# Bias products moved to the middle of an expert loop, and two late loads cut in halves

## The reference

```python
logits = (x2d @ w_router) + b_router
top_logits, top_idx = lax.top_k(logits, TOP_K)
gates = jax.nn.softmax(top_logits, axis=-1)
gu = xe @ w_gu[e] + b_gu[e]            # 1024 x 2048 per expert
g = jnp.minimum(gu[:, :D_FF], 7.0)
u = jnp.clip(gu[:, D_FF:], -7.0, 7.0)
h = (u + 1) * (g * jax.nn.sigmoid(1.702 * g))
y = h @ w_down[e] + b_down[e]          # 1024 x 1024 per expert
out = zeros.at[row_token].add(y * gate)
```

## Time and profile before

| | |
|---|---|
| median of three runs | 1069.88 us |
| profiled execution | 1070.29 us |
| its span | 1068.5 us |
| PE busy | 1024.9 us, 96% |
| DVE busy | 331.3 us, 31% |
| ACT busy | 92.6 us, 9% |
| from HBM | 418.29 MB |
| PE waiting for weights of `w_gu` | 32.1 us in 16 waits |

### The profile page before, as it was taken

The page is one execution under the profiler, slowest core; times in us unless marked ns, Lnnn a source line. Parts: engine busy times, 40 slices in busy tenths (PEclk is TensorE's granted clock), DMA queues, the critical chain, the costliest instruction groups (busy, mean ns, idle before and its releaser), DMA issues.

```text
span 1068.5 us, 11798 instructions
## 1 busy us (share of the span) xinstructions
PE 1024.9 (96%) x5098; PEld 490.2 (46%) x5099; DVE 331.3 (31%) x571; ACT 92.6 (9%) x162; POOL 8.3 (1%) x20
## 2 busy tenths in 40 slices
PE   9999999999999999989898989989898989999998
PEld 7767454444444444444343534344343435334333
DVE  3533031243323232323223241323223232413243
ACT  2222030010000000000000010100000000100001
POOL 1100000000000000000000000000000000000000
PEclk9999999999999999999999999999999999999999
DMA  9970969999999999999999999999999999999996
GB/s 351 302 193 3 370 255 401 421 421 411 418 425 429 428 424 429 428 426 430 429 426 429 429 427 429 429 427 429 429 427 429 428 427 429 427 416 420 421 420 240
DMA packets 60499, 420.39 MB, mean 393 GB/s; under 512 B 21396, under 2 KB 21712, under 8 KB 28848
## 3 DMA queue, kind: packets, MB, share of 16 engines
q1 hardware_dynamic: 59872, 419.32, 95.1%
q0 software_dynamic: 352, 0.55, 0.2%
q10 hardware_dynamic: 240, 0.03, 0.0%
HBM read 418.29 MB, written 1.58 MB: 393 GB/s over the span
## 4 chain that ended last, share of the span: by engine, by line
PE 74%; DMA 25%; SPq 0%; issue 0%; DVE 0%; ACT 0%; DVEq 0%
PE ps L911 36%; DMA ring<-in_w_gu_dram 25%; PE ps L927 9%; PE ps L837 8%; PE ps L759 5%; PE ps L953 4%; PE ps L777 3%; PE ps L635 2%; PE ps L938 1%; PE ps L913 1%; PE ps L788 1%; PE ps L957 1%; PE ps L1089 1%; PE ps L661 1%; PE ps L727 0%; PE ps L704 0%
## 5 line engine op out<-in xcount | busy, mean ns | idle before, releaser
L911 PE MATMUL ps<-ring,xT 128*64 128x512 f32 x1008 | 451.9, 602 | 32.1 <-DMA ring<-in_w_gu_dram 31.8
L913 PE MATMUL ps<-ring,xT 128*64 128x512 f32 x1000 | 449.2, 602 | 0.0
L911 PEld LDWEIGHTS ps<-ring,xT 128*64 128x64 f32 x1008 | 134.8, 138 | 303.1 <-issue 298.8
L927 PE MATMUL ps<-ring,he 128*64 128x512 f32 x472 | 210.3, 595 | 3.6 <-DMA ring<-in_w_down_dram 2.8
L929 PE MATMUL ps<-ring,he 128*64 128x512 f32 x472 | 210.8, 596 | 0.0
L1675 DVE TENSOR_TENSOR acc<-ps,acc 128x512 f32<-128x512 f32 (+1 forms) x78 | 50.4, 684 | 276.2 <-PE ps L953 248.5
L913 PEld LDWEIGHTS ps<-ring,xT 128*64 128x64 f32 x1000 | 133.8, 138 | 0.0
L927 PEld LDWEIGHTS ps<-ring,he 128*64 128x64 f32 x472 | 61.9, 137 | 131.4 <-issue 131.2
L837 PEld LDWEIGHTS ps<-oh,x 128*128 128x128 f32 x768 | 95.3, 196 | 10.3 <-issue 7.4
L837 PE MATMUL ps<-oh,x 128*128 128x128 f32 x768 | 97.9, 283 | 0.0
L1318 ACT COPY gu_sb<-ps 128x1024 f32<-128x1024 f32 x16 | 16.2, 1012 | 585.1 <-PE ps L913 585.1
(11 more groups left out here) (236 smaller groups left out, 645.2 us busy)
## 6 DMA issues: line engine op xcount, KB each, us to landing
ring<-in_w_gu_dram SPq DMA_DIRECT2D x86, 2048.0 KB, 27.0
ring<-in_w_down_dram SPq DMA_DIRECT2D x46, 2048.0 KB, 27.0
ring<-in_w_gu_dram SPq DMA_DIRECT2D x79, 1024.0 KB, 11.3
ring<-in_w_down_dram SPq DMA_DIRECT2D x32, 1024.0 KB, 24.4
w_chc<-in_w_in_dram SPq DMA_DIRECT2D x1, 4096.0 KB, 21.8
w_qkv<-in_w_in_dram SPq DMA_DIRECT2D x4, 768.0 KB, 9.2
w_b<-in_w_in_dram SPq DMA_DIRECT2D x1, 2048.0 KB, 29.2
w_o<-in_w_out_dram SPq DMA_DIRECT2D x2, 1024.0 KB, 27.7
```

The costliest lines, as they stand in the source:

```text
L911: even = mm(gu_banks(j)[0:CAP, n, :], xT[j % 2][:, k, 0:CAP], first[n], start=(k == 0), stop=(k == KT - 1))
L913: odd = mm(gu_banks(j)[CAP:P, n, :], xT[j % 2][:, k, CAP:P], second[n], start=(k == 0), stop=(k == KT - 1))
L927: even = mm(out[0:CAP, half, :], hid[:, f, 0:CAP], first[2 * a + half], start=(f == 0), stop=(f == FT - 1))
```

## The change

The bias products go from passes 14 and 15 to passes 8 and 9 (`BIASED_AT` is 8), with the transposes of the gates, the copy on ScalarE and the load of `b_dn`. The two spare places that held chunks for passes 14 and 15 now hold both first chunks of expert 16, used in pass 8; the chunks (28, 0) and (30, 0) come through the ring. PE's loop becomes two loops of two turns, over passes 4 to 7 and 10 to 13, with passes 8 and 9 written out between them. The second and third down steps of pair 15 (m = 1 and 2) get their weights in row halves of 4 KB: the first halves of both experts' chunks, then the second halves. `down` waits for the first halves (`fronts_in`), does its first two of four column blocks, and then waits for the rest.

```diff
-        BIASED = {PAIRS - 4: (2, 3, 4, 5), PAIRS - 3: (0, 1)}
+        BIASED_AT = PAIRS // 2
+        BIASED = {BIASED_AT - 2: (2, 3, 4, 5), BIASED_AT - 1: (0, 1)}
...
-        EARLY_AT, LATE_AT, PIECES_AT = (1, CH - 1), (NE - 2, 0), (NE - 4, 0)
+        EARLY_AT, LATE_AT, PIECES_AT = (1, CH - 1), (2 * BIASED_AT, 1), (2 * BIASED_AT, 0)
...
-            two = (FIRST_TWO <= n < RINGED + 1 - FINE and c % 2 == 0 and ORDER[n + 1] == (e, c + 1)
+            two = (FIRST_TWO <= n < RINGED - FINE and c % 2 == 0 and ORDER[n + 1] == (e, c + 1)
...
-            for first, many in LOADS[RING:]:
+            for first, many in LOADS[RING:-2 * len(fronts_in)]:
                 sp.wait_ge(chunk_used, max(used_up_to(*ORDER[n - RING]) for n in range(first, first + many)))
                 load(*ORDER[first], many, slot_of(first))
+            for m, fronts in fronts_in.items():
+                both = [RINGED - 2 * (DNC - m) + s for s in range(2)]
+                sp.wait_ge(chunk_used, max(used_up_to(*ORDER[n - RING]) for n in both))
+                for a in range(FPC):
+                    for s, n in enumerate(both):
+                        sp.dma_start(ring[:, slot_of(n), a * D:(a + 1) * D],
+                                     rows_of(*ORDER[n], 1)[:, a * D:(a + 1) * D]
+                                     ).then_inc((fronts[s], chunk_in[slot_of(n)])[a], 16)
...
-            def down(j, m, hid=he, out=Y):
+            def down(j, m, hid=he, out=Y, fronts=()):
                 first, second = PLACE[(2 * j, GUC + m)], PLACE[(2 * j + 1, GUC + m)]
-                landed(j + 1, 2 * j, GUC + m)
-                landed(j + 1, 2 * j + 1, GUC + m)
+                for front in fronts:
+                    pe.wait_ge(front, 16)
                 for a in range(FPC):
+                    if a == len(fronts) // 2:
+                        landed(j + 1, 2 * j, GUC + m)
+                        landed(j + 1, 2 * j + 1, GUC + m)
...
-            IN_LOOP, PER_LOOP = range(4, PAIRS - 2), 2 * 2 * CH
+            LOOPS, PER_LOOP = (range(4, BIASED_AT), range(BIASED_AT + 2, PAIRS - 2)), 2 * 2 * CH
...
-                down(L, m, he_last, Y_LAST)
+                down(L, m, he_last, Y_LAST, fronts_in.get(m, ()))
```

More of the change, by code:

```diff
@@ L276, in hybrid_layer_kernel @@
         acc_in, marks_in = sem("acc_in"), sem("marks_in")
+        fronts_in = {m: [sem(f"fronts_in{m}{s}") for s in range(2)] for m in (1, 2)}
         last_in, front_down, front_yh, front_yl = (sem(n) for n in ("last_in", "front_down", "front_yh", "front_yl"))
@@ L511, in _ @@
                 sp.dma_start(pieces_chunk[n], rows_of(*PIECES_AT, 1)[:, n * 512:(n + 1) * 512]).then_inc(pieces_in, 16)
-            for first, many in LOADS[RING:]:
+            for first, many in LOADS[RING:-2 * len(fronts_in)]:
                 sp.wait_ge(chunk_used, max(used_up_to(*ORDER[n - RING]) for n in range(first, first + many)))
                 load(*ORDER[first], many, slot_of(first))
+            for m, fronts in fronts_in.items():
[3 more added lines that the diff above has]
+                    for s, n in enumerate(both):
+                        assert ORDER[n] == (NE - 2 + s, GUC + m)
+                        sp.dma_start(ring[:, slot_of(n), a * D:(a + 1) * D],
+                                     rows_of(*ORDER[n], 1)[:, a * D:(a + 1) * D]
+                                     ).then_inc((fronts[s], chunk_in[slot_of(n)])[a], 16)
             sp.wait_ge(chunk_used, max(used_up_to(*ORDER[n - RING]) for n in (RINGED - 2, RINGED - 1)))
@@ L968, in chunks_of @@
                     [(2 * j - 2 + s, c) for s in range(2) for c in range(GUC, CH)]
-            for j in IN_LOOP[2:]:
-                for (e, c) in chunks_of(j):
+            for loop in LOOPS:
+                for (e, c) in [at for j in loop[2:] for at in chunks_of(j)]:
                     told, value = LANDED[(e - 4, c)]
@@ L974, in _, with growing @@
                     assert LANDED[(e, c)] == (told, value + PER_LOOP // RING * 16)
[L975 to L979, removed]
-            def so_far(j, value, step):
[L982 to L986, removed]
+            def growing(loop):
+                arrivals = sorted({LANDED[at][1] for j in loop[:2] for at in chunks_of(j)})
+                return ([(loop[0] + a, 2) for a in range(-1, 4)]
+                        + [(2 * NT * (loop[0] - 2) + value, 2 * 2 * NT) for value in range(2, 2 * 2 * NT + 1, 2)]
+                        + [(value, PER_LOOP // RING * 16) for value in arrivals])
+            regs = [pe.alloc_register(f"so_far_{i}") for i in range(max(len(growing(loop)) for loop in LOOPS))]
+            def so_far(j, value, step):
+                for loop in LOOPS:
+                    if j in loop:
+                        return regs[growing(loop).index((value, step))]
+                return value
             def rest_of_front():
@@ L1009, in pair @@
                     gate_up(j, k, rest_of_front if j == 0 and k == 0 else None)
-                    if j == PAIRS - 2 and k == 0:
+                    if j == BIASED_AT and k == 0:
                         turn_gates()
@@ L1030, in pair @@
                             pe.wait_ge(yl_ready, so_far(j, j - 1, 2))
-                            if j == PAIRS - 2:
+                            if j == BIASED_AT:
                                 pe.wait_ge(gatesT_ready, 1)
                         else:
-                            if j == PAIRS - 2:
+                            if j == BIASED_AT:
                                 pe.wait_ge(b_down_in, 16)
@@ L1069, in pair @@
                         turn_oh(so_far(j, j, 2))
[L1071 to L1076, removed]
-                    pair(j)
[L1078 to L1081, removed]
+            unrolled = 0
+            for loop in LOOPS:
+                for j in range(unrolled, loop[0]):
+                    pair(j)
+                for reg, (value, step) in zip(regs, growing(loop)):
+                    pe.reg_mov(reg, value)
+                with pe.Fori(0, len(loop) // 2):
+                    for j in loop[:2]:
+                        pair(j)
+                    for reg, (value, step) in zip(regs, growing(loop)):
+                        pe.reg_add(reg, reg, step)
+                unrolled = loop[-1] + 1
+            for j in range(unrolled, PAIRS):
                 pair(j)
```

## The result

The changed kernel takes 1071.14 us (median of 22 runs, 1070.29 to 1073.20), the kernel before, in 22 runs beside it, 1069.93 (1068.56 to 1071.36). The ratio is 1.0012, 95% interval 1.0007 to 1.0018: slower by 1.3 us. That is within the 0.2% that was called no change, but clear of zero, and it has the other sign than the forecast's -0.1 us.

The account below looks back on a forecast made before the run. PE's chain was taken to bound the end, the weights' chain 0.7 us behind. Terms -0.7 (PE), +0.1 (wait), +0.5 (code), 0 (loads) gave -0.1: 1069.8 us, range 1069.3 to 1071.3, 8 in 10 within 1067.6 to 1072.1.

Parts of the forecast that it names:

- What bounds the end: Last down steps: PE's chain sets the end, weights 0.7 us behind, so PE's chain can advance by 0.7 us.
- The sign that the last half step starts within 0.2 us of its landing: End of kernel: expected mark of the forecast, PE's last half step starting within 0.2 us of the last landing, near 1058.
- The cover in passes 8 and 9: Passes 8 and 9: 7.3 us of moved work covered by PE's 8.0 us idle and chunks lying ready; no cost at end.
- Halves: Last pair's second and third down steps: worth 0.1 us on PE, costing 0 to 0.8 us in the queues, 0.2 taken.
- rival C: Last steps: a wait brings the lower clock, +1.7 us, 1071.5; chance 0.12.
- signs of being wrong: Late kernel: no PE wait after 960, last landing moved over 1.5 us, or clock 0.50 in the last 15 us.
- Code: Passes 8 to 11: ten more instruction blocks delay everything behind by 0.4 to 1.1 us, 0.5 taken.
- Rival B: Weight queues: each code block delays the slowest engine 0.61 us, ten delay the last landing 6.1 us, 1075.4; chance 0.12.

Follow-up runs that it names:

- no bias products: Kernel before without the six bias products; transposes, bias load, loop, places and loads stay: 1069.24 us, ratio 0.9994.
- without halves: Changed kernel with whole chunks again for the second and third down steps of the last pair: 1071.07 us, ratio 1.0014.
- loops back to back: Kernel before with PE's loop split into passes 4 to 7 and 8 to 13, nothing written out between: 1070.31 us, ratio 1.0002.
- bias at pass 12: Changed kernel with bias products in passes 12 and 13, one loop over passes 4 to 11, no row halves: 1070.28 us, 1.0000 of before.
- two loops: Kernel before with only PE's loop divided, passes 4 to 7 and 10 to 13, 8 and 9 written out: 1071.97 us, ratio 1.0017.
- no loop: Kernel before with passes 4 to 13 written out, all else as before: 1073.64 us, ratio 1.0033.

## Why the prediction was wrong

The measured 1071.14 us lies within the stated range, but the forecast was -0.1 us and the change is +1.3, clear of zero. By the forecast's own steps:

- What bounds the end: right in the main. PE's chain sets it with a small lead; taking 6.9 us off it gave 0.6 (no bias products), and in the changed kernel PE waits 1.3 us at late steps. Which landing caps the gain was misread: not the last one but that of the first down step of pair 15, 15 us ahead (1042.02 without bias products, 1043.93 without halves). The sign that the last half step starts within 0.2 us of its landing came true only in the slowest execution. That the size fits, 0.7 for some 1.0 in the profile, is partly luck.
- The cover in passes 8 and 9: right. The bias work took 5.6 us of idle time between 600 and 718 and cost the end nothing that shows. The load of `b_dn` landed in time; the products began at 594.1. That it costs nothing holds only since it is paid once either way: 0.44 MB of weights before, 0.62 now.
- Halves: no effect that can be told, as forecast (1.0002, 1.0012 against 1.0014, 1.0114 against 1.0112, 0.9996 against 0.9994).
- The lower clock over the last steps (rival C): not seen; the waits there stayed at 1.3 us or less, and the granted clock was 1.00 from 976 to 1062. It is 0.50 from 1068.5, when PE's work is done, as before the change from 1067.0. Of the signs of being wrong one came up, in the slowest execution: the last landing stood 3.5 us later than before (1061.3 for 1057.8), 2.8 of which were there at pass 7.
- Code: this is the step that failed. Ten blocks were put at 0.5 us, by their bytes and by one pair of rates (427 and 429 GB/s; a third stretch, 441 to 559, also without blocks, has 428). The runs say 1.8 us for nine. A table, with the 0.7 us of PE's lead taken into account where the bias products no longer stand at the end:

| kernel | blocks more | change of time, us | moved landing, us | per block |
|---|---|---|---|---|
| loops back to back | 4 | +0.2 | 0.2 | 0.05 |
| bias at pass 12 | 4 | 0.0 | 0.7 | 0.18 |
| two loops | 9 | +1.8 | 1.8 | 0.20 |
| changed kernel | 9 | +1.3 | 2.0 | 0.22 |
| without halves | 9 | +1.5 | 2.2 | 0.24 |
| no loop | 17 | +3.5 | 3.5 | 0.21 |

The changes are the ratios times 1070, the blocks are those of the page over the 25 of before. The moved landing is worked out, not measured. In the kernels with the bias work in passes 14 and 15 PE waits for weights last at the third step of pass 14 and has next to no gap behind it, so the weights' delay goes into the time in full. In the three with the bias work moved PE has given up its lead, so the first 0.7 us of delay (0.6 by the run without bias products) don't show and are added. Each row has an interval of some 1 us to either side, so the rows with four blocks prove little alone; those with nine and 17 stand clear of both zero and 0.05 a block.

The two loops and no loop, which change the code alone, give 0.2 us a block. With it nine blocks are 1.8 us, and the forecast's sum reads -0.7+0.1+1.8+0 = +1.2 us, against +1.3 measured. The term was mis-sized by 1.3 us, and that is the error.

How a block costs 0.2 us is known in part. In the mean of the queue it costs 0.1 us: 0.31 MB for nine blocks and 0.77 for 18 are 0.08 and 0.10 us each, just the 0.1 that the forecast read from the rates and then halved. The rest isn't in the bytes. Rival B had a mechanism for it, a block that holds up the slowest engine, at 0.61 us a block, and was dismissed because five such blocks between 318 and 436 lowered the rate by 0.5% only. But a rate is a mean over all engines and can't show that one of them falls behind; the landings can. By their sixteen marks, the last mark falls back from the mean by 1.4 us at a time with a code block just before it: at 711 in the changed kernel, at 607 and 824 with no loop. Most blocks do nothing of the kind. So the mechanism of B is seen in single landings, at 1.4 us and seldom in place of 0.61 each time. That such jumps make up the whole of the other 0.1 us is argued and not shown, since one profile of each kernel holds too few of them, and they also come where all kernels have the same code: for the load that PE waits for at pass 7 the last mark is 3.1 us behind the mean in the changed kernel and 1.1 before, which is 2.0 of the 2.8 us by which that profile is late there.

What stays open is why some blocks cost 1.4 us and most nearly nothing, and whether it is the blocks or the written-out passes as such that count.

The lesson in the chances: the price was named as 0.4 to 1.1 us, with 6.1 as the rival's, and the value taken lay at the lower end of the range.

## What to carry to other kernels

Where a weight stream sets the end, written-out code is traffic of its own and here cost more than its bytes: before breaking a loop to move work, price the extra code blocks by a run that changes the loop alone. Taking work off an engine gains its lead over the next chain and no more; read that lead at every late step, not at the last landing alone. And where the stream sets an engine's start in the middle, a delay of the stream there isn't covered by a lead at the end. Work may be moved only to where the engine waits for the stream, not to where the stream waits for the engine: the same 7 us cost nothing in pass 8 and 12 us in pass 2.

## What the runs showed of the hardware

A block of 16 KB of PE's instructions, 0.04 us of the weights' bandwidth by its bytes, cost about 0.2 us of time on average (17 blocks: +3.5 us; nine: +1.8), of which the bytes that the weights' queue lost are half (0.77 MB and 0.31 MB from 440 to 925). In one case the landings of two loads of 2 MB were 6.5 us apart, 4.9 for their neighbours, with one block between; one of the sixteen marks of arrival had fallen back by 1.5 us. The load of `b_dn`, 128 KB, took 0.62 MB from the weights' queue within 12 us in the changed kernel and 0.44 MB before, with one of PE's code blocks in either stretch: three to four times the bytes of both. Loads of 512 KB with rows of 4 KB, eight behind one another on a full queue, made no difference that could be measured. The granted clock fell to 0.50, the lower of its two levels, for 3.4 us from 597.5 in the changed kernel, although PE had been busy without a gap since before 575; it had done the bias products and the gathering just before.
